# The order of the three products of a panel in a split-precision block on one core

## The chip, the cores and the metric

The kernel runs on one core of a Trainium2 chip, in one launch. The core has TensorE (matrix products, results in PSUM), VectorE, ScalarE, GpSimd and SyncE, each with its own in-order queue, and semaphores between them. The metric is device time in microseconds from the start to the end of the execution.

## The reference

Two transformer-like blocks over 512 tokens of width 1024, all in float32. The first has two layers: half a feed-forward block (width 2816), attention (latent attention in layer 0, a sparse attention with compressed, selected and window branches in layer 1) with a memory attention beside it, an output projection, another half feed-forward block, and a layer norm after each. The second block has an even layer (a bidirectional state-space model, a Fourier mix, gates) and an odd layer (average pooling, a short convolution, gates), and an RMS norm. Nearly all arithmetic is products with weights:

```python
def swiglu(x, w_gu, w_down):
    g, u = jnp.split(x @ w_gu, 2, axis=-1)
    return (jax.nn.silu(g) * u) @ w_down
# first block, per layer:
x = layer_norm(DN_ALPHA * x + 0.5 * swiglu(x, ffn_w_gu[layer, 0], ffn_w_down[layer, 0]), ...)
# ... mixer, output projection, second swiglu, then the second block:
xl = xl + gate[:, None] * out_l
```

## The kernel before

Activations lie transposed: channels on the 128 partitions, in 8 blocks of 128, and the 512 tokens along the row. A product with a weight matrix is cut into *panels*: 128 output channels of a matrix, over all its input channels, so 8 (in a few stages 6) weight tiles of 128 x 128, one per input block k, that add up in one PSUM bank of 512 columns. There are 385 panels in 16 stages (`STAGES`, `BASE`): `mem` 8, `ffn0` to `ffn3` 68 each, `mla` 6, `wo0` and `wo1` 8, `kv` 6, `nsa` 9, `ctx` 6 (256 columns), `even` 16, `glu` 6, `ewo` 8, `odd` 24, `owo` 8. A feed-forward stage has three chunks, each with its gate and up panels (16, 16, 12) and then 8 down panels; the first two chunks run in hardware loops of four panels, in which semaphore values are computed from the loop counter. Between parts of these stages stand fillings, small pieces of other work (`s5_fill`, line 965: transposes of matrices that GpSimd builds for the state-space model).

For float32 accuracy each operand is split in two parts, high and low. For inputs they are XH and XL (HH and HL within a feed-forward block, CH and CL in `ctx`, YH and YL for the mixers' outputs), for weights `wh` and `wl`. The product of the low parts is left out, so each k takes three products: `wh`·high, `wl`·high, `wh`·low.

A panel p passes through four engines:

- SyncE loads the weights into `raw[p % 4]` (line 599), when `w_lo` says that panel p - 4 is split.
- ScalarE writes `wh[p % 2]` (`cast`, line 1487), when `pe_panel` says that TensorE has finished panel p - 2, and counts `w_hi`.
- VectorE writes `wl[p % 2] = raw - wh` (`rest`, line 1978) and counts `w_lo`; in a few places GpSimd does it (`rests`, line 2713).
- TensorE does the products (`panel`, line 742) and counts `pe_panel`. ScalarE or VectorE then reads the bank and counts `taken`.

Each engine's order is written out. ScalarE and VectorE do their casts and rests between the work of norms, attention and scans, so a `wl` can come late.

On TensorE there are three writings. `pair` (line 758) does the first two panels of a stage together, k by k as the input arrives, with three products per k. `z_step` (line 1054) does three panels of `even` the same way, beside other work. `panel` does all others. Of these, 22 are given `need`, a semaphore to wait for at each k: the first of each four down panels (in the third chunk only the first), and the first panels of `mem` and `ctx`. `within` is the helper `running_sum` (line 846), four small products of a norm, called in the last panel of a stage before its last k.

Of the kernel before, what the change touches and what calls it, by code (L numbers as in the profile page):

```python
# [16 lines left out]
P = 128  # L17
# [147 lines left out]
def program(nc, A, C, out, scratch):  # L165

    ctx = ExitStack()
    with ctx:
        def sb(name, shape, dt=F32):
            return ctx.enter_context(nc.sbuf_tensor(name, shape, dt))  # L170

        def sem(name):
            return ctx.enter_context(nc.semaphore(name))
# [3 lines left out]
        wh = sb("wh", [P, 2, PAN], F32R)  # L177
        wl = sb("wl", [P, 2, PAN], F32R)
# [20 lines left out]
        ps = ctx.enter_context(nc.psum_tensor("ps", [P, 8, T], F32))  # L199
# [190 lines left out]
        w_hi = sem("w_hi")  # L390
        w_lo = sem("w_lo")
        pe_panel = sem("pe_panel")
# [336 lines left out]
        def _(pe):  # L729
            def panel(stage, j, i, hi, lo, nk=8, n=T, need=None, within=None):  # L730

                p = BASE[stage] + j
                pe.wait_ge(w_lo, p + 1 + 4 * i)
                if not (isinstance(i, int) and p + 4 * i < 4):
                    pe.wait_ge(taken[p % 4], p // 4 + i)
                for k in range(nk):
                    if need is not None:
                        pe.wait_ge(*need(k))
                    if within is not None and k == nk - 1:
                        within()  # L740
                    for a, (w, x) in enumerate(((wh, hi), (wl, hi), (wh, lo))):
                        mm = pe.matmul(ps[:, p % 4, 0:n], w[:, p % 2, k * P:(k + 1) * P], x[:, k, 0:n],  # L742
                                       start=(k == 0 and a == 0), stop=(k == nk - 1 and a == 2))
                mm.then_inc(pe_panel, 1)
# [33 lines left out]
            def panels(stage, count, need, hi=XH, lo=XL, nk=8, after=None):  # L778

                pair(stage, hi, lo, need, nk)  # L780
                for j in range(2, count):
                    panel(stage, j, 0, hi, lo, nk, within=(lambda: running_sum(stage)) if stage in SHIFT_AT and j == KD - 1 else None)
                    if after is not None:
                        after(j)
# [10 lines left out]
            def ffn(stage, fill):  # L795
# [4 lines left out]
                for c, nf in enumerate(CHUNKS):  # L800
                    for a, b in zip(UP_PARTS[c], UP_PARTS[c][1:]):
                        if c == 0:
                            pair(stage, XH, XL, split_at(stage))
                            for j in (2, 3):
                                panel(stage, j, 0, XH, XL)
                            a = 1
                        with pe.Fori(a, b) as i:
                            for j in range(4):
                                panel(stage, off + j, i, XH, XL)
                        fill(at)  # L810
                        at += 1
                    off += 2 * nf
                    need = lambda k: (h_ready, f0 + k + 3)
                    if c < 2:
                        with pe.Fori(0, KD // 4) as i:
                            for j in range(4):
                                panel(stage, off + j, i, HH, HL, nf, need=need if j == 0 else None)
                    else:
                        for j in range(KD):
                            panel(stage, off + j, 0, HH, HL, nf, need=need if j == 0 else None,  # L820
                                  within=(lambda: running_sum(stage)) if j == KD - 1 else None)
                            shift(stage, j)
                    if c < 2:
                        fill(at)
                        at += 1
                    off += KD
                    f0 += nf
# [251 lines left out]
            for k2 in range(4):  # L1079
                for e in range(2):  # L1080
                    for m in range(MT):
                        k = 2 * k2 + e
                        mm = pe.transpose(ps[:, 4 + k2, e * M + m * P:e * M + (m + 1) * P], MN[:, m, k * P:(k + 1) * P], IDENT[:])
# [24 lines left out]
            for layer in range(2):  # L1108
                for j in range(2):
# [4 lines left out]
                    for m in range(MT):  # L1114
                        mm = pe.transpose(ps[:, 4 + 2 * layer + j, m * P:(m + 1) * P], MV[:, 2 * layer + j, m * P:(m + 1) * P], IDENT[:])
# [11 lines left out]
            for n in range(12):  # L1127
                mm = pe.transpose(ps[:, 5 + n // 4, (n % 4) * P:(n % 4 + 1) * P], CN[:, n // 6, n % 6].rearrange("p d q -> p (d q)"), IDENT[:])
# [31 lines left out]
            for g in range(14):  # L1160
                if g < 6:
                    lhs, rhs, n = WUKV[:, 0, 2 * g:2 * g + 2, :].rearrange("p h c -> p (h c)"), CKV[:], T
                else:
                    t, half = (g - 6) // 2, g % 2
                    lhs, rhs, n = CKV[:, t * P:(t + 1) * P], WUKV[:, 1, 6 * half:6 * half + 6, :], 6 * HD
# [66 lines left out]
            for e in range(2):  # L1232
                pe.wait_ge(*taken_at("kv", 3 + 2 * e))
                for t in range(TT):
                    mm = pe.transpose(ps[:, 4 + e, t * P:(t + 1) * P], VT[:, e, t * P:(t + 1) * P], IDENT[:])
# [3 lines left out]
            for j in range(2):  # L1239
                pe.wait_ge(zb_ready, j + 1)  # L1240
                for m in range(2):
                    for l in range(CMP_LEN // 2):
                        mm = pe.matmul(ps[:, 6 + j, m * 2 * NCMP:(m + 1) * 2 * NCMP], W1[j][:, l, m * P:(m + 1) * P], ZB[:, j, l, :, 0:NCMP],
                                       start=l == 0, stop=l == CMP_LEN // 2 - 1)
# [124 lines left out]
            for t in range(TT):  # L1369
                for j in range(2):  # L1370
                    mm = pe.matmul(ps[:, 4 + t, j * 2 * P:(j + 1) * 2 * P], UB[:, j, t * P:(t + 1) * P], DFTC[:], start=True, stop=True)
                mm.then_inc(fnet_ps, 1)
            for j in range(2):
                pe.wait_ge(fnet_out, 4)
                for t in range(TT):
                    for e in range(2):
                        mm = pe.matmul(ps[:, 4 + j, :], FA[:, t, j, e * P:(e + 1) * P], DFTT[:, e, t, :],
                                       start=t == 0 and e == 0, stop=t == TT - 1 and e == 1)
# [90 lines left out]
            for d in range(KD):  # L1469
# [3 lines left out]
                for t in range(TT):  # L1473
                    mm = pe.transpose(ps[:, b, t * P:(t + 1) * P], XT[:, d, t * P:(t + 1) * P], IDENT[:])
# [1611 lines left out]
```

## Time and profile before

| | |
|---|---|
| median of 3 runs | 2726.3 us (2716.13 to 2727.91) |
| the profiled execution, its time | 2726.39 us |
| its span | 2724.6 us |
| TensorE busy, mean granted clock | 95% of the span, 0.966 |
| products, weight loads | 12898, 12898 |
| VectorE, ScalarE, GpSimd busy | 53%, 34%, 37% |

The span is from the first to the last instruction; the execution's own time is a little longer. The ends of TensorE's products are modelled: each product of 512 columns is shown as 0.39 us long while the next one starts 0.23 us after it, so in the timeline the starts count. An idle time stands only where the modelled end lies before the next start.

### The profile page before, as it was taken

To read this page: it belongs to the slowest core of one execution; us is meant where nothing else is said; L and a number is where in the kernel's file an instruction comes from. 1 tells how busy PE (TensorE), PEld (TensorE's weight loads), DVE (VectorE), ACT (ScalarE), POOL (GpSimd) and SP (SyncE) were. 2 spreads that over 40 slices of the span, in tenths; PEclk is the share of its full clock that TensorE was granted. 3 is DMA by queue.
4 is the path that set the end of the run, shared out by engine and by line. 5 is a ranking of instruction groups with operands and counts; after the bars stand their busy time and mean duration, and the time that the engine had idled before them with its cause. 6 is when DMAs were issued, how large, how long until landed. Compare 5 with 4: busy or idle time off the path is not lost.

```text
span 2724.6 us, 35186 instructions
## 1 busy us (share of the span) xinstructions
PE 2587.1 (95%) x12898; PEld 2114.2 (78%) x12898; DVE 1456.9 (53%) x2165; ACT 933.2 (34%) x1461; POOL 1015.5 (37%) x683
## 2 busy tenths in 40 slices
PE   7999999899999999999999989989999988988998
PEld 6877887578788887788878789878888866776786
DVE  5565556664655645444644567564333363794453
ACT  3222225443422223332212566453122243352222
POOL 1888865002748933224441411064012053020410
PEclk8999999998999999999999999999999988999999
DMA  7345445211434454244542311136333325333231
GB/s 182 93 118 150 121 120 143 72 26 39 122 117 129 150 141 117 85 131 124 154 123 85 106 36 36 61 108 157 108 109 102 89 88 153 127 127 108 78 93 62
DMA packets 439428, 291.96 MB, mean 107 GB/s; under 512 B 34867, under 2 KB 420714, under 8 KB 435850
## 3 DMA queue, kind: packets, MB, share of 16 engines
q1 hardware_dynamic: 422186, 212.38, 27.7%
q0 software_dynamic: 17120, 77.93, 9.4%
q8 instruction: 78, 1.28, 0.2%
q14 instruction: 44, 0.36, 0.0%
HBM read 272.50 MB, written 20.92 MB: 108 GB/s over the span
## 4 chain that ended last, share of the span: by engine, by line
PE 74%; DVE 9%; POOL 6%; ACT 4%; issue 3%; DMA 2%; SPq 1%; DVEq 0%; ACTq 0%; POOLq 0%
PE ps L742 56%; PE ps L758 4%; PE ps L910 2%; DVE wl L1978 2%; ACT wh L1487 2%; POOL NS L2759 1%; POOL SW L2761 1%; PE ps L901 1%; POOL NS L2758 1%; PE ps L919 1%; PE ps L1266 1%; PE ps L1071 1%; PE ps L1037 1%; DMA raw<-in_ffn_w_gu 1%; PE ps L1054 1%
## 5 line engine op out<-in xcount | busy, mean ns | idle before, releaser
L1978 DVE TENSOR_TENSOR wl<-raw,wh 128x1024 fp32r<-128x1024 f32 x376 | 623.0, 1657 | 974.0 <-ACT wh L1487 971.3
L1487 ACT ACTIVATE wh<-raw 128x1024 fp32r<-128x1024 f32 x385 | 408.1, 1060 | 1410.0 <-PE ps L742 1313.0
L742 PE MATMUL ps<-XH,wh 128*128 128x512 f32 x1848 | 727.6, 394 | 14.0 <-DVE wl L1978 14.0
L742 PE MATMUL ps<-XL,wh 128*128 128x512 f32 x1848 | 719.9, 390 | 0.0
L742 PE MATMUL ps<-XH,wl 128*128 128x512 f32 x1848 | 719.7, 389 | 0.0
L742 PEld LDWEIGHTS ps<-XH,wh 128*128 128x128 f32 x1848 | 347.3, 188 | 98.1 <-DVE wl L1978 22.0
L742 PEld LDWEIGHTS ps<-XH,wl 128*128 128x128 f32 x1848 | 347.4, 188 | 72.8 <-issue 2.2
L742 PEld LDWEIGHTS ps<-XL,wh 128*128 128x128 f32 x1848 | 347.2, 188 | 72.9
L742 PE MATMUL ps<-HH,wh 128*128 128x512 f32 x704 | 282.1, 401 | 9.1 <-DVE HL L1997 8.6
L742 PE MATMUL ps<-HH,wl 128*128 128x512 f32 x704 | 279.2, 397 | 0.0
L742 PE MATMUL ps<-HL,wh 128*128 128x512 f32 x704 | 277.9, 395 | 0.0
L2858 POOL TENSOR_TENSOR NS<-AW,CS 128x2048 f32<-128x2048 f32 x32 | 116.0, 3625 | 235.4 <-PE ps L985 225.9
L742 PEld LDWEIGHTS ps<-HH,wh 128*128 128x128 f32 x704 | 134.1, 191 | 45.2 <-DVE HL L1997 11.8
L2721 POOL COPY ACC<-XT 128x512 f32<-128x512 f32 x6 | 3.7, 611 | 438.4 <-DVE XT L2039 438.4
L742 PEld LDWEIGHTS ps<-HL,wh 128*128 128x128 f32 x704 | 133.9, 190 | 29.2
L742 PEld LDWEIGHTS ps<-HH,wl 128*128 128x128 f32 x704 | 134.0, 190 | 28.9 <-issue 1.0
L1661 ACT ACTIVATE PR<-PR,NB 128x128 f32<-128x128 f32 (+3 forms) x144 | 79.1, 550 | 92.4 <-DVE NB L2249 92.4
L758 PE MATMUL ps<-XH,wh 128*128 128x512 f32 x188 | 84.5, 449 | 20.4 <-ACT XH L1567 10.7
L2859 POOL TENSOR_TENSOR NS<-NS 128x1024 f32<-128x1024 f32 x32 | 101.6, 3176 | 2.5
L2919 POOL DMA_DIRECT2D BS<-s_b x12 | 6.6, 553 | 235.5 <-PE ps L1037 180.5
L1997 DVE TENSOR_TENSOR HL<-HF,HH 128x512 f32 x88 | 83.1, 944 | 11.4 <-DVE HF L1995 1.0
L758 PE MATMUL ps<-XH,wl 128*128 128x512 f32 x188 | 80.3, 427 | 0.0
(476 smaller groups left out, 3766.8 us busy)
## 6 DMA issues: line engine op xcount, KB each, us to landing
raw<-in_ffn_w_gu SPq DMA_DIRECT2D x176, 512.0 KB, 3.8
raw<-in_ffn_w_down SPq DMA_DIRECT2D x64, 512.0 KB, 4.1
AW<-in_ada_w POOLq DMA_DIRECT2D x24, 1024.0 KB, 6.9
raw<-in_ffn_w_down SPq DMA_DIRECT2D x32, 384.0 KB, 3.5
BS<-s_b POOLq DMA_DIRECT2D x12, 1024.0 KB, 6.8
raw<-in_odd_w_in SPq DMA_DIRECT2D x24, 512.0 KB, 3.7
raw<-in_even_w_in SPq DMA_DIRECT2D x22, 512.0 KB, 4.0
raw<-in_w_out SPq DMA_DIRECT2D x16, 512.0 KB, 4.7
```

The source lines that it names most:

```text
L742: mm = pe.matmul(ps[:, p % 4, 0:n], w[:, p % 2, k * P:(k + 1) * P], x[:, k, 0:n], start=(k == 0 and a == 0), stop=(k == nk - 1 and a == 2))
L758: return pe.matmul(ps[:, (p + e) % 4, 0:n], w[:, (p + e) % 2, c * P:(c + 1) * P], x[:, c, 0:n], start=c == 0 and w is wh and x is hi, stop ...
L901: mm = pe.transpose(ps[:, bank, col:col + P], PR[:, s, POFF[q] + kb * P:POFF[q] + (kb + 1) * P], IDENT[:])
L910: mm = pe.matmul(ps[:, 7, q * HD:(q + 1) * HD], PT[:, s, PTOFF[q, kb]:PTOFF[q, kb] + P], vals(kb), start=kb == 0, stop=kb == q)
L919: mm = pe.matmul(ps[:, bank, col:col + n], q(t), keys(n), start=True, stop=True)
L1037: mm = pe.matmul(ps[:, 6 + t % 2, (r * GT + g) * NCC:(r * GT + g + 1) * NCC], BS[:, t % 3, r, g, :], UC[:, t * GT + g, :], start=True, sto ...
L1487: act.activation(wh[:, p % 2, :], raw[:, p % 4, :], ACT.Copy).then_inc(w_hi, 1)
L1661: ins = act.activation(PR[:, s, POFF[t]:POFF[t] + (t + 1) * P], PR[:, s, POFF[t]:POFF[t] + (t + 1) * P], ACT.Exp, bias=NB[:, s, t:t + 1], ...
L1978: dve.tensor_tensor(wl[:, p % 2, :], raw[:, p % 4, :], wh[:, p % 2, :].bitcast(F32), ALU.subtract).then_inc(w_lo, 1)
L1997: dve.tensor_tensor(HL[:, k, :], HF[:, f:f + 1, :], HH[:, k, :].bitcast(F32), ALU.subtract).then_inc(h_ready, 1)
L2858: step(pool.tensor_tensor(prod, AW[:, n % 2], CS[:, :, e:e + 1].broadcast_to([P, KD, 2 * P]), ALU.mult))
L2859: step(pool.tensor_tensor(prod[:, 0:4], prod[:, 0:4], prod[:, 4:8], ALU.add))
```

## The change

Without `need`, the panel waits at its head for `w_hi` instead of `w_lo`, does all products with `wh` (for each k with the high, then the low input), then waits for `w_lo` and does the products with `wl` for all k. `within` is called before the last of these. With `need`, the order and the waits are as they were.

```diff
--- before.py
+++ after.py
@@ -730,14 +730,22 @@
             def panel(stage, j, i, hi, lo, nk=8, n=T, need=None, within=None):
 
                 p = BASE[stage] + j
-                pe.wait_ge(w_lo, p + 1 + 4 * i)
+                pe.wait_ge(w_lo if need is not None else w_hi, p + 1 + 4 * i)
                 if not (isinstance(i, int) and p + 4 * i < 4):
                     pe.wait_ge(taken[p % 4], p // 4 + i)
+                if need is None:
+                    for k in range(nk):
+                        for x in (hi, lo):
+                            pe.matmul(ps[:, p % 4, 0:n], wh[:, p % 2, k * P:(k + 1) * P], x[:, k, 0:n], start=k == 0 and x is hi, stop=False)
+                    pe.wait_ge(w_lo, p + 1 + 4 * i)
+                    for k in range(nk):
+                        if within is not None and k == nk - 1:
+                            within()
+                        mm = pe.matmul(ps[:, p % 4, 0:n], wl[:, p % 2, k * P:(k + 1) * P], hi[:, k, 0:n], start=False, stop=k == nk - 1)
+                    mm.then_inc(pe_panel, 1)
+                    return
                 for k in range(nk):
-                    if need is not None:
-                        pe.wait_ge(*need(k))
-                    if within is not None and k == nk - 1:
-                        within()
+                    pe.wait_ge(*need(k))
                     for a, (w, x) in enumerate(((wh, hi), (wl, hi), (wh, lo))):
                         mm = pe.matmul(ps[:, p % 4, 0:n], w[:, p % 2, k * P:(k + 1) * P], x[:, k, 0:n],
                                        start=(k == 0 and a == 0), stop=(k == nk - 1 and a == 2))
```

## Rows read from the trace of the kernel before

**Rows 1.** The page: busy time of the engines, and the chain that ended last.

```profile
PE 2587.1 (95%) x12898; PEld 2114.2 (78%) x12898; DVE 1456.9 (53%) x2165; ACT 933.2 (34%) x1461; POOL 1015.5 (37%) x683
...
PE 74%; DVE 9%; POOL 6%; ACT 4%; issue 3%; DMA 2%; SPq 1%; DVEq 0%; ACTq 0%; POOLq 0%
```

**Rows 2.** Waits of TensorE: line, waited for: us in total, times, longest us.

```profile
PE ps L742 <- DVE wl L1978: 19.3, 23, 3.0
...
PE ps L742 <- POOL wl L2713: 2.6, 2, 1.7
```

**Rows 3.** Timeline: start, us, engine, line, out<-in, count [idle before <-releaser].

```profile
710.48 1.06 ACT L1487 ACTIVATE wh<-raw 128x1024 fp32r<-128x1024 f32 x1 [0.50 <-PE ps L758]
...
711.57 1.23 DVE L1978 TENSOR_TENSOR wl<-raw,wh 128x1024 fp32r<-128x1024 f32 x1 [2.17 <-ACT wh L1487]
...
712.10 0.39 PE L758 MATMUL ps<-XL,wh 128*128 128x512 f32 x1
...
712.86 0.50 PE L742 MATMUL ps<-XH,wh 128*128 128x512 f32 x1 [0.37 <-DVE wl L1978]
```

**Rows 4.** Timeline: panel 2 of mla, even and odd, with ScalarE before the last.

```profile
475.45 0.50 PE L742 MATMUL ps<-XH,wh 128*128 128x512 f32 x1 [1.08 <-DVE wl L1978]
...
2260.22 0.50 PE L742 MATMUL ps<-XH,wh 128*128 128x512 f32 x1 [0.95 <-DVE wl L1978]
...
2532.91 1.06 ACT L1487 ACTIVATE wh<-raw 128x1024 fp32r<-128x1024 f32 x1 [5.34 <-POOL PU L3041]
...
2535.28 0.50 PE L742 MATMUL ps<-XH,wh 128*128 128x512 f32 x1 [2.36 <-DVE wl L1978]
```

**Rows 5.** Timeline: waits of panels inside a stage, and one cast by ScalarE.

```profile
167.84 0.50 PE L742 MATMUL ps<-HH,wh 128*128 128x512 f32 x1 [0.31 <-DVE wl L1978]
...
729.81 0.50 PE L742 MATMUL ps<-XH,wh 128*128 128x512 f32 x1 [0.34 <-DVE wl L1978]
...
741.41 0.50 PE L742 MATMUL ps<-XH,wh 128*128 128x512 f32 x1 [0.42 <-DVE wl L1978]
...
1028.94 1.06 ACT L1487 ACTIVATE wh<-raw 128x1024 fp32r<-128x1024 f32 x1 [7.99 <-DMA raw<-in_ffn_w_gu]
...
1031.32 0.50 PE L742 MATMUL ps<-XH,wh 128*128 128x512 f32 x1 [1.06 <-DVE wl L1978]
...
1123.32 0.50 PE L742 MATMUL ps<-XH,wh 128*128 128x512 f32 x1 [0.97 <-DVE wl L1978]
...
1168.35 0.49 PE L742 MATMUL ps<-XH,wh 128*128 128x512 f32 x1 [0.17 <-DVE wl L1978]
```

**Rows 6.** Timeline of TensorE: panel 2 of ffn0, and that stage's first S5 filling.

```profile
74.71 0.50 PE L742 MATMUL ps<-XH,wh 128*128 128x512 f32 x1 [1.85 <-DVE wl L1978]
...
152.62 1.97 PE L965 MATMUL ps<-IDENT,BK 128*128 128x128 f32 x16 [1.46 <-POOL SW L2820]
```

**Rows 7.** Timeline, stage ctx: ScalarE's cast of a panel, and the longer wait of TensorE.

```profile
1813.93 1.04 ACT L1487 ACTIVATE wh<-raw 128x1024 fp32r<-128x1024 f32 x1
...
1818.18 0.38 PE L742 MATMUL ps<-CH,wh 128*128 128x256 f32 x1 [1.75 <-POOL wl L2713]
```

**Rows 8.** Timeline: panel 13 of even, VectorE behind it, and the first wait of ewo.

```profile
2384.67 0.50 PE L742 MATMUL ps<-XH,wh 128*128 128x512 f32 x1 [1.54 <-DVE wl L1978]
...
2397.08 1.23 DVE L1978 TENSOR_TENSOR wl<-raw,wh 128x1024 fp32r<-128x1024 f32 x1 [0.29 <-ACT wh L1487]
...
2464.05 0.50 PE L758 MATMUL ps<-YH,wh 128*128 128x512 f32 x1 [0.34 <-DVE YL L2658]
```

**Rows 9.** Timeline of TensorE: first products of panels 20, 21 and 22 of ffn2.

```profile
1259.22 0.39 PE L742 MATMUL ps<-HH,wh 128*128 128x512 f32 x1
...
1264.71 0.39 PE L742 MATMUL ps<-HH,wh 128*128 128x512 f32 x1
...
1270.20 0.39 PE L742 MATMUL ps<-HH,wh 128*128 128x512 f32 x1
```

**Rows 10.** Weight loads of line 846, grouped: count, busy, mean ns, idle before.

```profile
L846 PEld LDWEIGHTS ps<-NS,ONES 128*32 128x32 f32 x288 | 6.0, 113 | 17.2 <-ACT NS L1528 8.4 <-issue 6.7 <-POOL NS L2731 2.0
```

## The prediction, made before the changed kernel ran

> **What bounds the kernel now.** Four views, in this order. The page's busy shares first [rows 1]: TensorE is busy 95% of the span, VectorE 53%, and the chain that ended last runs 74% through TensorE. The rest of the chain goes through the other engines only where TensorE waits. So what can be won without removing products is TensorE's waits. Then the waits of TensorE by line [rows 2]: line 742, the product of the helper `panel`, waited 19.3 us for `wl` from VectorE in 23 places and 2.6 us for `wl` from GpSimd in 2. These are all the waits that this change can touch directly. Then the timeline of one such wait, to see what the time consists of [rows 3], and the timeline of the others, to see what follows each of them.
>
> How a wait reads in rows 3. Panel 2 of `ffn1` follows the pair. ScalarE writes its `wh` from 710.48 to 711.54, VectorE its `wl` from 711.57 to 712.80, and TensorE starts at 712.86. Its last product before that began at 712.10. Where TensorE is not waiting, a product begins 0.229 us after the one before (24 in 5.49 us, rows 9), so it would have gone on at 712.33. The stall is 0.53 us: the 0.37 us of the row and 0.16 us that the modelled end (0.39 us) overstates against the step of 0.23 us. I add that 0.16 us to every idle time below. `wh` had landed at 711.54, before 712.33, so a panel that asks for `wh` alone has no stall here.
>
> **The change, part by part.**
>
> First, the wait at the head of 332 panels is for `wh` instead of `wl`. The 332 are 385 panels less 28 in pairs, 3 in the written-out steps of stage `even`, and 22 that take input k by k. What each stall turns into:
>
> (a) Panel 2 behind a pair, the pattern of rows 3. Five have 0.37 or 0.38 us in their row (`ffn1`, `ffn2`, `ffn3`, `ewo`, `owo`), four have 0.43 us (`wo0`, `kv`, `nsa`, `wo1`); with the 0.16 that is 2.67 + 2.36 = 5.0 us. In `mla` and `even` the row has 1.08 and 0.95 us [rows 4]; `wh` had landed before TensorE was free there too, which gives 1.24 + 1.11 us. In `odd` the row has 2.36 us, but `wh` itself ends only at 2533.97 [rows 4], so TensorE starts at about 2534.03 instead of 2535.28: 1.25 us. Sum of (a): 8.6 us.
>
> (b) Inside a stage, where VectorE came to `wl` late, behind other work in its queue: 0.31, 0.34, 0.42, 1.06, 0.97 and 0.17 us [rows 5], with 0.16 each 4.2 us. In the fourth, `wh` waited for its transfer, was begun at 1028.94 and ended at 1030.00 [rows 5]; the start moves from 1031.32 to about 1030.06, so it counts in full.
>
> (c) What goes away and comes back as another wait. Panel 2 of `ffn0` (2.0 us) [rows 6]: the next filling of that stage already waits 1.46 us for GpSimd at 152.62, on a chain that hangs on nothing of TensorE's after the start; TensorE will wait 3.5 us there. The 3.0 us wait of the memory panels [the longest in rows 2] shrinks by 1.3 us, but the next panels of that stage hang on loads. In `ctx`, two waits for GpSimd, 2.6 us together and 1.75 us the longer [rows 2, 7], 2.9 us with the 0.16 each: ScalarE is not waiting when it writes the `wh` of the following panel at 1813.93, it works through its queue, so the start of `ffn3` behind it does not move. Panel 13 of `even` (1.70 us) [rows 8]: VectorE runs its scan without a gap but for 0.29 us before the next `wl`, and TensorE later waits for the end of that scan; 0.3 us stays. Panel 2 of `glu` (0.6 us): the next stage starts when VectorE has written the last YL [rows 8], and VectorE has no gap between the two. Of these 8.5 us I keep 0.3.
>
> Sum of the first part: 8.6 + 4.2 + 0.3 = 13.1 us less. If everything in (c) stayed won it would be 21.3 us.
>
> Second, the products with `wl` stand last, behind a new wait for `wl`. In front of them are 16 products of 0.229 us, 3.66 us (1.9 us in `ctx`, with half the columns). In the worst place, panel 2 of `ffn0`, `wl` ends 1.9 us after the moment at which the panel can now start (its stall, as `wh` was there); in `ctx` it is the 1.9 us of its longer stall, just covered; elsewhere less. So the new wait is met in every panel when TensorE reaches it. Queued behind it are the eight last products, and for them wait the reader of the bank and the next `wh`, which may overwrite its buffer once the panel is counted. What a met wait costs by itself: the panels that take their input k by k have eight such waits each, and one whose waits are long met (1259.22 to 1264.71, 5.49 us) is as long as the next without any (1264.71 to 1270.20, 5.49 us) [rows 9]. That is the end at zero. The other end is the first product after a wait that was not met, 0.50 us long instead of 0.39 [rows 3]: 0.11 us in 332 panels, 36 us. I take zero, since rows 9 are the same kind of wait, in the same helper, on the same engine.
>
> Third, the order itself. The count of products and of weight loads is the same, as is the work per panel. But `wh` of one k is now used twice in a row. The step of 0.229 us is 0.0155 us more than 512 columns at 2.4 GHz (0.2133 us). If a repeated weight saved that, it would be 8 products in each of 332 panels, about 40 us; if alternating the input cost as much again, 40 us the other way. I take zero: there are as many weight loads as products in the whole trace [rows 1], and line 846, which uses the same ONES columns four times running, shows 288 loads for its 288 products [rows 10].
> The same page of the Trainium skill, same section, says that weights can be loaded once and multiplied repeatedly. That is the rule which would make the 40 us come; the rows say that here the program loads for each product.
>
> Fourth, `running_sum` stands before the last product instead of before the last three, 0.46 us later in the panel. The panel ends at the same time; zero. Loads: SyncE waits for `wl` as before, and nothing of it is moved.
>
> **The sum.** The profiled execution took 2726.39 us, 1.8 us around its span of 2724.6; the median of the runs shown is 2726.3. 2726.4 - 13.1 = 2713.3 us. 0.5% is 13.6 us, about what a measurement of this kernel can tell from no change; the forecast lies on that line.
>
> **The rivals.**
> 1. The in-order engines give more of it back: `wh` and `wl` come from ScalarE and VectorE, and where these set the pace a stall taken from TensorE comes back one wait later, as in (c). For it: half of the touched waits lie near norms and mixers, where both are loaded. Against: in (a) and in `ffn` TensorE runs on for many panels without a wait. If (b) and a third of (a) go too, 6 us stay: 2720 us.
> 2. All of it stays won, (c) too: 21 us, 2705 us. Against: the wait for GpSimd in rows 6.
> 3. Repeated weights are cheaper: 40 us more, 2673 us. Against: rows 1 and 10.
> 4. Slower: the new wait in the middle of a panel stops the stream each time. Place: 332 panels; price: up to 0.11 us each; it outweighs the gain from 13.1 / 332 = 0.04 us on. At full price the kernel takes 2713 + 36 = 2749 us. Against: rows 9.
> 5. It does not do what it says: `wh` comes as late as `wl`, because the split in ScalarE is what is late. In `odd` and the memory panels this is half true; in the other rows `wh` is there. Left would be the 1.25 us of `odd` and the 1.24 us of `mla`: 2724 us.
>
> **How the numbers follow.** Forecast 0.62, rival 1 0.18, rival 2 0.08, rival 3 0.03, rival 4 0.05, rival 5 0.04. The forecast's own range is 2706 to 2720, since the three runs before lie 12 us apart. For 8 in 10 the range takes in rival 1 and most of rival 2: 2703 to 2723. Faster by over 0.5%: slightly under half of the forecast (0.29), rivals 2 and 3 and the lower edge of the others, 0.42. Slower by over 0.5%: rival 4, 0.05. Within: 0.53.
>
> **What would show it.** In the waits of TensorE by line, the products that replace line 742 should wait for `wl` about 0 us, and some 3 us for `wh` (the memory panel and `odd`). The idle time at the first S5 filling should grow from 1.46 to about 3.5 us, that before the `ffn3` pair by about 2.9 us. An ordinary full panel should stay at 5.45 to 5.49 us; 5.6 would mean rival 4, under 5.3 rival 3. The forecast is wrong if the new wait shows tens of waits with the `wl` as releaser, or if the waits for HL, XL and GpSimd together grow by over 10 us.

## The result, and the profile after

The changed kernel took 2699.2 us (median of 6 executions, 2697.4 to 2707.2) against 2724.7 us for the kernel before in the same comparison: ratio 0.9904, 95% interval 0.9877 to 0.9932. The forecast was 2713.3 us, its range 2703 to 2723. So the kernel is faster, by more than forecast, and the time lies under the range. The profiled execution took 2699.34 us, with a span of 2697.5 us and a mean granted clock of 0.971 (before: 2726.39, 2724.6 and 0.966). One further execution of the kernel before, of 5861.02 us, is left out as slow from every figure of the batches below.

The page of the changed kernel, busy times and chain, answers to [rows 1]:

```profile
PE 2564.9 (95%) x12898; PEld 2103.9 (78%) x12898; DVE 1456.5 (54%) x2165; ACT 933.4 (35%) x1461; POOL 1015.0 (38%) x683
...
PE 76%; DVE 8%; POOL 6%; ACT 4%; issue 3%; DMA 2%; SPq 1%; DVEq 0%; ACTq 0%; POOLq 0%
```

There are as many products and weight loads as before. PE's busy time is 22.2 us shorter for the same work. That alone says that not all of the difference is idle time.

The waits of TensorE by line, of the changed kernel (us in total, times, longest), answer to [rows 2]. Line 739 is now the product with `wh`, 744 the product with `wl`, 750 the products of panels with `need`, 766 the pair, 973 the S5 filling:

```profile
PE ps L739 <- ACT wh L1495: 2.2, 2, 1.1
...
PE ps L744 <- POOL wl L2721: 1.0, 1, 1.0
...
PE ps L750 <- DVE HL L2005: 8.6, 5, 2.3
...
PE ps L750 <- DVE wl L1986: 1.2, 1, 1.2
...
PE ps L766 <- DVE wl L1986: 6.3, 2, 5.3
...
PE ps L973 <- POOL SW L2828: 5.4, 3, 3.8
```

The 19.3 us for `wl` from VectorE are gone but for 1.2 us at the first panel of `mem`, which has `need`. For `wh` there are 2.2 us, at panel 57 of `ffn1` and panel 2 of `odd`. Line 744 waits once, in `ctx`, and nowhere for VectorE. Two kinds of waits grew where the prediction said. The first S5 filling (line 973) went from 1.46 to 3.84 us. The waits of the pairs for `wl` were one before,

```profile
PE ps L758 <- DVE wl L1978: 3.5, 1, 3.5
```

that of the `ffn3` pair, and are two in the changed kernel:

```profile
1820.63 0.79 PE L766 MATMUL ps<-XH,wh 128*128 128x512 f32 x1 [5.34 <-DVE wl L1986]
...
2436.19 0.50 PE L766 MATMUL ps<-YH,wh 128*128 128x512 f32 x1 [0.96 <-DVE wl L1986]
```

The first is the `ffn3` pair, whose wait grew by 1.9 us (2.9 were predicted). The second is the `ewo` pair, where the gain of panel 2 of `glu` comes back.

The timeline of the changed kernel around panel 2 of `ffn1` answers to [rows 3]:

```profile
708.11 1.06 ACT L1495 ACTIVATE wh<-raw 128x1024 fp32r<-128x1024 f32 x1 [0.18 <-PE ps L766]
...
709.21 1.23 DVE L1986 TENSOR_TENSOR wl<-raw,wh 128x1024 fp32r<-128x1024 f32 x1 [1.85 <-ACT wh L1495]
...
709.75 0.39 PE L766 MATMUL ps<-XL,wh 128*128 128x512 f32 x1
709.98 0.39 PE L739 MATMUL ps<-XH,wh 128*128 128x512 f32 x1
...
713.60 1.98 PE L744 MATMUL ps<-XH,wl 128*128 128x512 f32 x8
```

`wh` ends at 709.17, and the panel starts at 709.98, one step of 0.23 us after the last product of the pair. `wl` ends at 710.44 and is asked for at 713.60. The prediction read this stall as 0.53 us. The kernel before pays more than that: after the stalled first product of rows 3, at 712.86, its timeline goes on with

```profile
713.19 0.39 PE L742 MATMUL ps<-XH,wl 128*128 128x512 f32 x1
713.42 0.39 PE L742 MATMUL ps<-XL,wh 128*128 128x512 f32 x1
```

so the first product holds the engine 0.33 us instead of 0.23 us. The stall costs 0.53 + 0.10 us. It is so throughout: behind every 512-column stall for `wl` or HL that the kernel before has at the full clock, the next product starts 0.33 to 0.34 us after the stalled one. I had the 0.11 us longer product in rows 3 before me and used it only as the upper end for another price.

The timeline of the changed kernel in `ffn2` answers to [rows 9]: two panels in the new order (their last eight products are the rows of x8), then one with `need`:

```profile
1244.21 1.99 PE L744 MATMUL ps<-HH,wl 128*128 128x512 f32 x8
...
1249.70 1.99 PE L744 MATMUL ps<-HH,wl 128*128 128x512 f32 x8
1251.53 0.39 PE L750 MATMUL ps<-HH,wh 128*128 128x512 f32 x1
...
1260.69 1.99 PE L744 MATMUL ps<-HH,wl 128*128 128x512 f32 x8
```

From one row of x8 to the next is 5.49 us, as before. Over the panel with `need` it is 10.99 us for two. Neither the order nor the met wait costs or saves anything here, so rivals 3 and 4 are out.

The first S5 filling of `ffn0` in the changed kernel answers to the second row of [rows 6], and the next row is its second half:

```profile
151.62 3.68 PE L973 MATMUL ps<-IDENT,BK 128*128 128x128 f32 x16 [3.84 <-POOL SW L2828]
155.23 2.75 PE L980 MATMUL ps<-SW,BB 128*16 128x240 f32 x32
```

It starts 1.0 us earlier than before (152.62), and it takes 3.68 us instead of 1.97. Behind the longer wait the granted clock is lower. These are the windows of 10 us around it (columns: window, its length, busy time and count of PE, PEld, DVE, ACT, POOL, granted clock, DMA share, GB/s), before and after:

```profile
150.62:160.62 10.00, 8.54 (x70) 6.29 (x69) 4.44 (x6) 4.40 (x7) 4.25 (x6) 1.00 0.35 105
```

```profile
149.62:159.62 10.00, 8.00 (x55) 5.73 (x56) 4.83 (x6) 2.71 (x5) 2.24 (x4) 0.66 0.18 52
```

It goes with the change of this one panel: in all six profiles of this document whose panel 2 of `ffn0` starts early, the filling waits 3.7 to 4.3 us and its 16 products take 2.8 to 3.7 us; in the seven others it waits 1.5 us or not at all, and they take 1.9 to 2.0 us. From cast 4 to cast 20 of `ffn0` it is 4.4 us longer, which takes back more than the 2.1 us that its panel 2 had won.

The `ffn3` pair is the second place where the change makes a stretch slower. In the 20 us from 5 us before its start the granted clock is 0.91 in the profile before and 0.83 in that after. Of the ten profiles in which the pair waits 5.3 us nine have 0.83 there and one 0.91; the two in which it waits 3.5 us have 0.91, and the one in which it waits 1.9 us has 1.00.

### The profile page after: what moved, and what is told of

Its sections match the earlier page's. It is cut to its first block, busy times and chain, and to the rows that moved or that the text cites. A ratio compares the mean times of both kernels' runs of the same rounds, so it can differ in the third digit from the quotient of the medians.

```text
span 2697.5 us, 35186 instructions
## 1 busy us (share of the span) xinstructions
PE 2564.9 (95%) x12898; PEld 2103.9 (78%) x12898; DVE 1456.5 (54%) x2165; ACT 933.4 (35%) x1461; POOL 1015.0 (38%) x683
## 4 chain that ended last, share of the span: by engine, by line
PE 76%; DVE 8%; POOL 6%; ACT 4%; issue 3%; DMA 2%; SPq 1%; DVEq 0%; ACTq 0%; POOLq 0%
PE ps L739 36%; PE ps L744 18%; PE ps L766 5%; PE ps L750 3%; PE ps L918 2%; POOL NS L2767 1%; POOL NS L2766 1%; POOL SW L2769 1%; PE ps L909 1%; ACT wh L1495 1%; PE ps L927 1%; PE ps L1274 1%; DVE wl L1986 1%; DMA raw<-in_ffn_w_gu 1%; PE ps L1079 1%
## 5 line engine op out<-in xcount | busy, mean ns | idle before, releaser
L744 PE MATMUL ps<-XH,wl 128*128 128x512 f32 x1848 | 457.2, 389 | 0.0
L739 PE MATMUL ps<-HH,wh 128*128 128x512 f32 x552 | 219.5, 398 | 0.0
L739 PE MATMUL ps<-HL,wh 128*128 128x512 f32 x552 | 217.6, 394 | 0.0
L744 PE MATMUL ps<-HH,wl 128*128 128x512 f32 x552 | 139.7, 392 | 0.0
L739 PEld LDWEIGHTS ps<-HH,wh 128*128 128x128 f32 x552 | 104.8, 190 | 24.0 <-issue 1.0
L739 PEld LDWEIGHTS ps<-HL,wh 128*128 128x128 f32 x552 | 104.8, 190 | 23.9 <-issue 1.0
L744 PEld LDWEIGHTS ps<-HH,wl 128*128 128x128 f32 x552 | 103.7, 188 | 23.4 <-issue 0.8
L766 PE MATMUL ps<-XH,wh 128*128 128x512 f32 x188 | 85.0, 452 | 22.2 <-ACT XH L1575 10.7
L766 PE MATMUL ps<-XH,wl 128*128 128x512 f32 x188 | 80.8, 430 | 0.0
```

What stands on the lines that cost most here:

```text
L739: pe.matmul(ps[:, p % 4, 0:n], wh[:, p % 2, k * P:(k + 1) * P], x[:, k, 0:n], start=k == 0 and x is hi, stop=False)
L744: mm = pe.matmul(ps[:, p % 4, 0:n], wl[:, p % 2, k * P:(k + 1) * P], hi[:, k, 0:n], start=False, stop=k == nk - 1)
L766: return pe.matmul(ps[:, (p + e) % 4, 0:n], w[:, (p + e) % 2, c * P:(c + 1) * P], x[:, c, 0:n], start=c == 0 and w is wh and x is hi, stop ...
```

## The experiments

The time of one kernel moves with the granted clock. In the batches below the kernel before took 2710.6 to 2740.9 us, at mean granted clocks of 0.975 to 0.963. Within each kernel the time falls by 2.27 us for each 0.001 of mean clock (one slope for 182 executions). "At 0.969" means a kernel's mean time brought to that clock by this slope, with its standard error.

Two things limit these figures. First, the four batches of the changed kernel (six, seven, ten and twelve executions) stand at 2706.4 ± 1.0, 2701.9 ± 0.6, 2705.0 ± 0.5 and 2705.6 ± 0.6 us, further apart than the errors allow. The ± count only the scatter of executions, so a difference of 2 to 3 us between kernels of different batches is not clear. Second, where a kernel itself lowers the clock, as at the filling above, bringing it to equal clock hides that cost.

Behind the result there are three batches, on three chips. The medians of the kernel before in them are 2721.9, 2722.9 and 2721.7 us. The first has the order alone, high then low, and behind pairs only; the second all but behind pairs, and the two with ffn0's panel 2 as before; the third the far places only and the interleaved panels. Each has the changed kernel once.

| kernel | executions | median | ratio, 95% interval | mean clock | at 0.969 |
|---|---|---|---|---|---|
| before | 74 | 2721.9 | | 0.9686 | 2721.9 ± 0.4 |
| changed, four batches | 35 | 2702.3 | in each text | 0.9687 | 2704.8 ± 0.4 |
| order only | 10 | 2729.5 | 1.0025, 1.0001 to 1.0050 | 0.9666 | 2722.8 ± 0.7 |
| high then low | 6 | 2704.5 | 0.9935, 0.9903 to 0.9968 | 0.9673 | 2702.4 ± 0.3 |
| behind pairs only | 10 | 2710.7 | 0.9948, 0.9928 to 0.9968 | 0.9711 | 2714.1 ± 0.9 |
| all but behind pairs | 12 | 2717.1 | 0.9989, 0.9961 to 1.0016 | 0.9661 | 2714.5 ± 0.4 |
| far from pairs only | 12 | 2724.7 | 1.0003, 0.9979 to 1.0027 | 0.9664 | 2718.0 ± 0.7 |
| ffn0 panel 2 as before | 10 | 2701.5 | 0.9920, 0.9894 to 0.9947 | 0.9700 | 2703.3 ± 0.4 |
| the same, with 16 products more | 8 | 2698.1 | 0.9918, 0.9889 to 0.9946 | 0.9725 | 2708.2 ± 0.8 |
| down panels interleaved | 5 | 2694.5 | 0.9885, 0.9854 to 0.9917 | 0.9690 | 2694.6 ± 0.6 |

**The changed kernel again**, three times more, beside other batches of the kernel before.

> The changed kernel itself, again, beside the kernel before on the same chip. Of the 27.0 us between the two profiled executions some 13 us are stalls taken away and some 14 us are TensorE time at the lower clock level (mean granted clock 0.966 before, 0.971 after, times the span). Theory A (the clock part belongs to the change, because TensorE's stalls and the times of the fillings moved): again about 25 us faster, with the changed kernel's mean clock above that of the kernel before. Theory B (the clock part is chance of one execution): the difference shrinks towards 13 us, and the clocks of the two kernels overlap.

> The changed kernel once more, for the statistics of its clock. 24 executions of the kernel before have a mean clock of 0.9686 and a median of 2721.9 us, 13 of the changed kernel have 0.970 and about 2701 us. If the clock is chance from one execution to the next, both kernels show the same mean clock over all runs, within 0.001, and at equal clock the changed kernel is 15 to 18 us faster; if the change keeps the clock up, its mean clock stays above by 0.0015 or more.

> The changed kernel again, beside the same runs of the kernel before. For the equal-clock comparison: 17 to 18 us less than before at the same mean granted clock. If the change also raises the clock, the mean granted clock over its executions is above that of the kernel before by 0.001 or more, as in two batches of three so far; if not, the two means agree to 0.0005. The median is about 2702 us.

The medians were 2701.5 (ratio 0.9926, 0.9905 to 0.9948), 2702.3 (0.9931, 0.9908 to 0.9953) and 2713.8 us (0.9960, 0.9933 to 0.9986), at mean clocks of 0.9687, 0.9699 and 0.9662. The last batch is 12 us slower than the others for the same program. Over all 35 executions the mean clock is 0.9687 ± 0.0006, against 0.9686 ± 0.0003 before. So no effect of the change on the mean clock shows, and the 0.005 by which the two first profiles differ is within what one program shows by itself. At equal clock the change saves 17.1 ± 0.6 us. The mean of the 35 is 2705.5 us, that of the 74 is 2722.8 us: 17.2 us without any correction for the clock. Each of the three batches by itself gives 19.2, 17.8 and 16.2 us at equal clock. The last batch missed its expected median of about 2702 us.

**The order alone.** The new order, with both halves behind one wait at the head:

```diff
-                pe.wait_ge(w_lo if need is not None else w_hi, p + 1 + 4 * i)
+                pe.wait_ge(w_lo, p + 1 + 4 * i)
```

> The new order of products, but the panel still waits at its head for wl, as before. Theory A (the earlier start is what pays, and whatever the clock gives back follows from it): no faster than the kernel before, within 5 us. Theory C (the order itself pays, in the step between products or in the clock): 10 to 25 us faster. The step between products in a full panel stays at 0.227 to 0.229 us by theory A.

At equal clock it is 0.9 ± 0.8 us above the kernel before, and it waits for `wl` at the head as the kernel before does (17.7 us in 22 waits, row of the waits of that kernel):

```profile
PE ps L739 <- DVE wl L1986: 17.7, 22, 2.3
```

Moving the products is worth nothing; asking for `wl` later is worth everything.

**All high inputs first, then all low inputs**, so that `wh` of one k is not used twice in a row:

```diff
-                    for k in range(nk):
-                        for x in (hi, lo):
+                    for x in (hi, lo):
+                        for k in range(nk):
```

> As the changed kernel, with the same early start, but all products wh x high input stand first, then all wh x low, so that the same weight tile is never used twice running. If the equal neighbours matter, this loses against the changed kernel (up to 14 us by the clock, more by the step). If only the early start matters, it is within 4 us of the changed kernel, about 25 us faster than before.

There is no loss from giving up the repeated weight: 2702.4 against 2704.8 us at equal clock. The 2.4 us the other way are no gain: the changed kernel of the same batch stands at 2701.9 ± 0.6.

**Only panel 2 of each stage** (term (a), with ffn0 and `glu`), and **all but these**. The first condition takes in panel 2 of `mem` and `ctx` too; the second kernel has `not (j == 2 and isinstance(i, int))` in its place:

```diff
+                early = need is None and j == 2 and isinstance(i, int)
-                pe.wait_ge(w_lo if need is not None else w_hi, p + 1 + 4 * i)
+                pe.wait_ge(w_hi if early else w_lo, p + 1 + 4 * i)
-                if need is None:
+                if early:
```

> Only panel 2 of each stage, the one behind the pair (and panel 2 of the first and the context stage), has the new order and the early wait; all other panels are as before. By the sum of the prediction this is term (a), 8.6 us, so 2716 us beside 2725. If the clock follows from the stalls taken away inside the long stages, the clock part is missing here; if it comes with any shift, the time is lower by more than 8.6 us.

> The complement of the run in which only panel 2 was changed: here panel 2 of each stage is as before and all other panels have the new order and early wait. By the prediction's sum this is terms (b) and (c), 4.5 us; with 0.11 us more for each stall (the first product after a wait is 0.50 us long, not 0.39) and 0.8 us more in stage even, about 6 us. If the two halves add up, this and the 11.3 us measured for the other half make the 20 us of the whole: then 9 us. So 2713 to 2717 beside 2722 by theory; under 2708 would mean that the two halves share their gain.

At equal clock they save 7.8 ± 1.0 and 7.4 ± 0.6 us. By the raw medians the one looks worth 11 us and the other 6, because their mean clocks were 0.9711 and 0.9661. Without the clock beside the times, these two would have led to the wrong term. The waits of TensorE in the first of them:

```profile
PE ps L754 <- DVE wl L1990: 7.2, 10, 1.5
PE ps L754 <- POOL wl L2725: 2.7, 2, 1.8
PE ps L770 <- DVE wl L1990: 2.3, 2, 1.9
```

Line 754 is the old order and 770 the pair. The waits behind pairs are gone, those inside stages and in `ctx` stay, and the pair of `ffn3` does not wait longer than before (1.9 us). The growth there in the changed kernel comes from `ctx`.

**Only mem, ctx, glu and the later panels of even** (term (c) without ffn0):

```diff
+                early = need is None and (stage in ("mem", "ctx", "glu") or (stage == "even" and j > 2))
```

> One part of the change alone: the new order only in mem, ctx, glu and the panels of even from 3 on, the places of term (c) without ffn0. The prediction kept 0.3 us of their 6.5 us. By the two profiles even 13 keeps about 1.1 us and ctx about 1 us, so 2 to 3 us less than before at the same mean granted clock (ratio about 0.999). If the part of the gain at equal clock that the sum does not explain (about 4 us) lies here, it is 6 us less (ratio about 0.9978). If it lies in the feed-forward stages, this kernel is within 1 us of what the prediction said, 0.3 us less.

It saves 3.9 ± 0.8 us at equal clock, where the prediction kept 0.3. Its profiled execution is 2.2 us shorter than the first one, but unrounded its clock is 0.9665 against 0.9657, which is 1.8 us by the slope. So the whole spans of these two say little, and the places have to be looked at one by one:

- **The memory panels.** At the first cast of `ffn0` the ten profiles whose later memory panels start early are 1.0 to 2.8 us ahead of the kernel before, 1.9 us on average. The two others are 0.8 and 0.6 us ahead. Some 1.2 to 1.9 us stay.
- **Panel 13 of `even`.** Cast 15 is 1.9 us earlier, which is before the wait for the scan. From the last product ahead of panel 13 to the first of the `glu` pair it is 54.90 us before (2382.74 to 2437.64), and 53.87 to 53.93 in the four profiles of the changed kernel: 1.0 us stays. In the profile of this kernel it is 53.17 us; there the clock is low in front of a wait for a transfer, where it costs less.
- **Panel 2 of `glu`.** The 0.75 us that it wins are given back at the `ewo` pair.
- **`ctx`.** The casts stand 0.4 us behind the kernel before all through `ctx`, and so does the start of the `ffn3` pair, at 1827.98 against 1827.56. Nothing is won. Behind it 1.0 us is lost, in the stretch with the granted clock of 0.83 instead of 0.91.

Two rows of its waits show that the pairs wait as in the full change, and that `ctx` is where a `wl` is late:

```profile
PE ps L770 <- DVE wl L1990: 6.3, 2, 5.3
PE ps L745 <- POOL wl L2725: 1.0, 1, 1.0
```

**ffn0's panel 2 as before, all else changed**:

```diff
+                early = need is None and (stage, j) != ("ffn0", 2)
```

> The changed kernel with panel 2 of ffn0 back in its old order, with its old wait for wl. There the stall taken away (2.0 us) came back at the first S5 filling, whose wait grew from 1.46 to 3.84 us, and the filling behind it took 3.68 us instead of 1.97, at the lower clock. Theory A (a stall moved in front of a longer wait is worse than nothing, since it lets the clock fall): wait back near 1.5 us, the filling back near 1.97 us, and 2 to 4 us faster than the changed kernel. Rival (the two stalls add to the same, the clock falls anyway): within 1 us of the changed kernel.

The timeline of TensorE in this kernel, at the first filling:

```profile
149.66 1.91 PE L977 MATMUL ps<-IDENT,BK 128*128 128x128 f32 x16
151.49 1.81 PE L984 MATMUL ps<-SW,BB 128*16 128x240 f32 x32
```

No wait is listed, and both halves run at the clock of before: 3.72 us instead of 6.43. In the two kernels below that also have this panel as before, the wait is 1.47 us and the 16 products take 1.97 us, as in the kernel before. The gain over the changed kernel is 1.5 ± 0.6 us at equal clock. That comparison cannot count the slow filling itself, since it corrects for the clock that the filling loses. The plain means are 2701.1 ± 2.1 and 2705.5 ± 1.4 us (2703.0 ± 1.8 for the changed kernel of the same batch). So the loss of 2.3 us (the 4.4 us less the 2.1) is shown by the traces, and the times agree with it but are too scattered to show it.

**The same with 16 products of 512 columns more** in the last fillings of `ffn3`, into a bank that nobody reads, to see whether they pay for themselves in clock:

```diff
+                        if t < 4 and g % 4 == 0:
+                            pe.matmul(ps[:, 5, :], XH[:, 0, 0:P], XH[:, 1, :], start=True, stop=True)
```

> As the one with panel 2 of ffn0 put back, and with 16 products of 512 columns more, four in each of the four fillings of ffn3, between their groups of four 32-column products; their results are not used. They cost 16 x 0.23 = 3.7 us. In the profile before the clock fell after three of the four fillings, 1.6 us each, in those after in none or one. If the fillings' few columns let the clock fall, the clock stays at 1.00 from the first filling to the end of ffn3, and the mean clock is 0.001 to 0.002 higher; the time is then within 2 us of the kernel without them. If the fillings have nothing to do with it, it is 3.7 us slower.

At equal clock they cost 4.9 ± 0.9 us (16 x 0.229 is 3.7). The mean clock was 0.0025 ± 0.0013 higher, which would give back 5.7 us. The medians are 3.4 us apart. In its profile the clock is 1.00 through the fillings of `ffn3`, but so it is in the profile of the kernel without them, and in two of the four of the changed kernel. This is inconclusive: the next batch of the changed kernel moved by more than that with nothing changed.

**A version beyond the change**, built on the kernel with ffn0's panel 2 as before. What TensorE still waits for in the down panels is the HL of the last input block (8.6 us in 5 waits, unchanged by the change). Here the first two down panels of each chunk are interleaved, so that 12 products stand between the last block but one and the last. The fifth down panel of the first two chunks no longer takes its input k by k and has the new order:

```diff
+                open_(0)
+                steps(0, range(nf - 1))
+                open_(1)
+                steps(1, range(ahead))
+                steps(0, (nf - 1,)).then_inc(pe_panel, 1)
+                steps(1, range(ahead, nf)).then_inc(pe_panel, 1)
```

> A version beyond the change. The products are those of the kernel with ffn0 panel 2 in the old order; new is that the first two down panels of each chunk of a feed-forward stage are interleaved: all input blocks but the last of down panel 0, then four blocks of down panel 1, then the last block of panel 0, then the rest of panel 1. The last input block's HL is what TensorE still waits for in the changed kernel: 8.6 us in 5 waits of the down panels that take their input k by k, up to 2.3 us each. Between the last block but one and the last one there are now 12 products, 2.75 us, that need nothing late. Theory: the 8.6 us of idle time go, with 0.11 us for each restart some 9 us, less what the first products of panel 1 wait for its own wl; the waits for HL become 0, the median is about 2692 us, ratio to before about 0.9885. Rival: VectorE and ScalarE set the pace of these stretches (they also write wh and wl for panel 1, which is now asked for 2.3 us earlier), so the time comes back as waits for wl of panel 1 or wh of panel 2, and the time is that of the changed kernel, about 2701 us.

The median is 2694.5 us. At equal clock it is 8.7 ± 0.7 us under its base, 10.2 ± 0.7 under the changed kernel and 27.3 ± 0.7 under the kernel before (11.0 and 27.2 us within its batch): the fastest of all, with five executions. The waits of TensorE in it have no row for HL any more. What there is for `wh` and `wl` in the panels is

```profile
PE ps L740 <- ACT wh L1528: 3.3, 3, 1.6
...
PE ps L754 <- DVE wl L2019: 2.8, 2, 1.6
```

Line 754 stands for the first `mem` panel and ffn0's panel 2, 740 for three panels that ask for `wh` (a memory panel, panel 57 of `ffn1`, panel 2 of `odd`). The theory held: the 8.6 us of idle time did not come back as a wait for the second panel, though `wl` of the second panel is asked for earlier.

## Why the prediction was wrong in size and right in mechanism

The step of the sum that failed is term (c), of which 0.3 us was kept and 3.9 ± 0.8 us stayed; and the price of every stall left out the slower product behind it. What bounds the kernel, what the early start wins and what order and middle wait cost were right. But the gain was only a part of the miss.

Forecast and result are 14.1 us apart. Three parts make 13.9 of it.

1. **The base, 3.6 us.** "2726.4 - 13.1 = 2713.3" starts from one execution at a mean clock of 0.966. The mean of 74 is 2722.8 us at 0.9686. The three times shown ahead (2716.13 to 2727.91) already spread by 12 us, and the page had the clock; I laid neither beside the other.
2. **The gain, 4.0 us.** 13.1 us were forecast; 17.1 ± 0.6 us it is at equal clock.
3. **The draw, 6.3 us.** The six executions of the result have a median of 2699.2 us, all 35 have a mean of 2705.5 us. The six had a mean clock of 0.9717; that they did is chance. The mean of the 35 lies inside the predicted range, but three of the four batches have medians under its lower end of 2703 us, so the miss is not chance alone.

The terms of the gain, at equal clock:

- **(a) behind pairs**: 8.6 us predicted, 7.8 ± 1.0 measured, with ffn0 and `glu` in it. The 0.11 us more for each stall, which I had left out, is 1.2 us here (11 places; in `odd` TensorE still waits). The loss in `ffn0` goes against it: without that panel the term is 7.8 + 1.5 = 9.3 us at equal clock. That `wh` is there in time held in all twelve places but `odd`, where TensorE waits 1.1 us for it, as the prediction had it.
- **(b) inside stages**: 4.2 us predicted; the kernel with all but panel 2, less the one with only the far places, gives 7.4 - 3.9 = 3.5 ± 1.0 us (8.3 - 3.8 = 4.5 with each beside the kernel before of its own batch), which does not differ from the prediction. Of the fourth of these stalls the prediction said "it counts in full". That depends on the execution: in the four profiles of the changed kernel panel 57 of `ffn1` waits 1.08, 0, 0.85 and 0.23 us for `wh`. In the profile of the result its transfer was issued 4.4 us earlier than before (1001.18 against 1005.58) and landed only 3.1 us earlier (1025.65 against 1028.75), since it took 24.5 us instead of 23.2.
- **(c) what comes back**: "Of these 8.5 us I keep 0.3." This is the step that failed. Outside `ffn0`, 3.9 ± 0.8 us stay at equal clock. In `mem` the prediction said "the next panels of that stage hang on loads" and kept nothing; some 1.2 to 1.9 us stay. In `even` it said that TensorE "later waits for the end of that scan; 0.3 us stays"; 1.0 us stays. For `glu` zero was right. In `ctx` "the start of `ffn3` behind it does not move" was right too: 1.0 us of the 2.9 is now waited for by line 744, and 1.9 us more by the pair. The lower clock behind it, 1.0 us, was not foreseen. These places make 2.2 to 2.9 us, without that loss, which the figure at equal clock hides. What is left to 3.9 is within the scatter of batches and stays open. In `ffn0` the prediction was too kind: the filling waits 3.84 us, 0.3 more than said, and then runs at a lower clock.
- (a) and the rest, each alone, sum to 15.2 ± 1.2 us, the whole change to 17.1 ± 0.6. The 1.9 us between are within what batches differ by, and not settled.

The middle wait costs zero, the order zero, the late `running_sum` nothing that shows; these were right, and they carried the forecast away from rivals 3 and 4. Full panels stayed at 5.49 us. `ctx` was "just covered": there line 744 waits 1.0 us, the one place where a new wait is met unready. Rival 1 (2720 us) and rival 5 (2724 us) are out. The 17.1 us lie midway between the forecast's 13.1 and the 21.3 of rival 2, in which all stays won; that rival is refuted in `ffn0` and `ctx` by the timeline, and half right in `mem` and `even`.

The first two profiles differ by 27 us, 10 us more than the change is worth. The stretches where they do are seen in the windows of the two kernels at the same work, the start of `even` (columns: window, its length, busy time and count of PE, PEld, DVE, ACT, POOL, granted clock, DMA share, GB/s). Before:

```profile
2302.00:2320.00 18.00, 17.54 (x65) 16.00 (x66) 6.26 (x10) 3.68 (x6) 0.53 (x1) 0.50 0.49 146
```

After:

```profile
2286.00:2304.00 18.00, 18.00 (x101) 16.47 (x100) 7.80 (x13) 6.55 (x10) 1.06 (x2) 0.78 0.50 145
```

Both come out of a wait for the transfer of U (9.3 and 10.1 us), at the level of 1.2 GHz. The one is still there at the end of the window; the other is back at 2.4 GHz in it. That the change decides which level such a stretch gets is not shown: in the kernel with the order alone, which wins nothing, the 40 us after this wait have a granted clock of 0.86, against 0.71 in the profile of before and 0.89 in that of after. Over the 13 profiles it goes from 0.71 to 0.92, with 0.82 in the other three of the changed kernel.

The Trainium skill (TensorE: Matmul & The Clock Gate, "Part 2: What happens when you issue a matmul") has the rule on weights loaded once that the prediction weighed. The traces do not show it here: 12898 loads stand beside 12898 products in the kernel with the repeated weight and in the one with the alternating weight. What a product without a load of its own would take, no run here shows.

## What to carry to other kernels

Let a product wait for an operand only where it reads it. In an in-order queue a wait that is met is free, and sixteen products of cover were enough for every late `wl` but one. When pricing a stall, add the slower first product behind it to the idle time. Before a forecast of a few tenths of a per cent, ask at which granted clock the profiled execution ran, and compare kernels at the same clock. When a gain is written off because another engine sets the pace later, bound it from both sides: here some 3.9 of 6.5 us outside `ffn0` stayed at equal clock, where 0.3 was kept. And a comparison at equal clock must not be used for the cost of a clock that the change itself lowers.

## What the runs showed of the hardware that was not expected

- The mean granted clock of one and the same program went from 0.960 to 0.974 over 35 executions (2728.9 to 2693.5 us), and batches of 10 and 12 executions, on two chips, differed by 12 us in their medians.
- The first product after an unmet wait takes 0.10 us more to the next one (712.86 to 713.19, where the step is 0.23; 0.33 to 0.34 in all such stalls of 512 columns at the full clock). It is not in the idle time of any row.
- A wait of 3.84 us for GpSimd was followed by small products at half the clock, 3.68 us for the 16 that take 1.91 without the wait. A wait of 1.46 us was not. Six profiles have the longer wait and seven the shorter or none, without an exception.
- One and the same transfer of 512 KB, the weights of panel 57 of `ffn1`, took 22.8 to 24.9 us over 13 profiles (23.2 before, 24.5 after), where the median of its kind is 3.8 us. Two transfers of 1 MB that GpSimd issues (W from `in_cmp_w`) were under way beside it.
